# Page loads moved to GpSimd's queue, and memory values projected by token with 512-column weights

## What is computed

```
x = x + 1/2 * SwiGLU_1(RMSNorm(x))
z = RMSNorm(x) @ w_in            # queries, keys, values, gates of three branches
A: attention over paged keys and values (8 heads of 128; each sample has 8 pages of 128 rows)
B: retention (4 heads of 256, a state for each sample)
C: attention into 256 memory tokens (4 heads of 256)
x = x + (sum over branches of sigmoid gate * branch @ w_br) @ w_out
x = x + 1/2 * SwiGLU_2(RMSNorm(x));  y = RMSNorm(x)
```

## Time and profile before

| | |
|---|---|
| median of 3 runs | 2739.36 us |
| the profiled execution | 2738.88 us |
| its span, first to last instruction | 2736.5 us |
| PE busy | 2683.8 us (98%) |
| DVE, ACT, POOL busy | 56%, 40%, 1% |
| granted TensorE clock, mean | 0.994 |
| moved by DMA | 601.19 MB, 220 GB/s |

### The profile page before, as it was taken

How to read it: one execution, slowest core, us unless ns; L and a number is a source line. 1 busy time by engine, 2 the same in 40 slices (tenths; PEclk the granted TensorE clock), 3 DMA queues, 4 the chain that set the end, 5 groups by cost and what they waited for, 6 DMA issues and landing times.

```text
span 2736.5 us, 51767 instructions
## 1 busy us (share of the span) xinstructions
PE 2683.8 (98%) x22179; PEld 2624.4 (96%) x22179; DVE 1540.7 (56%) x2467; ACT 1094.4 (40%) x967; POOL 36.6 (1%) x66
## 2 busy tenths in 40 slices
PE   7999999999999999999997999999999999999998
PEld 7999999999999999998997988899999999999997
DVE  4545554455447778776773744355555555555455
ACT  6433333333335433554452444344433333333345
POOL 0000000000000000000000000000000000000000
PEclk9999999999999999999999999999999999999999
DMA  7575555555555788799987799756555555555553
GB/s 241 179 254 179 184 185 183 178 178 184 185 168 162 237 294 299 251 355 365 324 305 265 268 310 315 279 170 213 173 182 184 183 179 178 183 185 184 177 158 113
DMA packets 502045, 601.19 MB, mean 220 GB/s; under 512 B 12608, under 2 KB 471584, under 8 KB 500576
## 3 DMA queue, kind: packets, MB, share of 16 engines
q1 hardware_dynamic: 485104, 559.08, 62.6%
q0 software_dynamic: 6528, 25.91, 2.6%
q10 hardware_dynamic: 10240, 13.70, 1.4%
HBM read 575.16 MB, written 25.58 MB: 220 GB/s over the span
## 4 chain that ended last, share of the span: by engine, by line
PE 92%; DVE 3%; DMA 3%; ACT 1%; issue 0%; SPq 0%; POOL 0%; DVEq 0%; ACTq 0%; POOLq 0%
PE PS L497 30%; PE PS L498 29%; PE PS L499 29%; DVE splitL L457 2%; DMA ring<-cache_k 1%; PE PS L1845 1%; DMA ring<-cache_mem_k 1%; DMA raw<-w_gate 1%; PE PS L1364 1%; ACT splitH L451 0%; PE PS L1619 0%; PE PS L1587 0%; DMA grow<-b_gate 0%; PE PS L1228 0%; PE PS L1114 0%
## 5 line engine op out<-in xcount | busy, mean ns | idle before, releaser
L457 DVE TENSOR_TENSOR splitL<-raw,splitH 128x2048 fp32r<-128x2048 f32 (+1 forms) x464 | 1011.9, 2181 | 831.0 <-ACT splitH L451 829.8
L451 ACT ACTIVATE splitH<-raw 128x2048 fp32r<-128x2048 f32 (+1 forms) x464 | 847.7, 1829 | 1519.6 <-PE PS L499 1507.4
L497 PE MATMUL PS<-gH,splitH 128*128 128x264 f32 x3072 | 883.0, 287 | 1.8 <-DVE splitL L457 1.8
L498 PE MATMUL PS<-gL,splitH 128*128 128x264 f32 x3072 | 872.8, 284 | 0.0
L499 PE MATMUL PS<-gH,splitL 128*128 128x264 f32 x3072 | 872.5, 284 | 0.0
L497 PEld LDWEIGHTS PS<-gH,splitH 128*128 128x128 f32 x3072 | 580.9, 189 | 21.0 <-issue 20.6
L498 PEld LDWEIGHTS PS<-gL,splitH 128*128 128x128 f32 x3072 | 581.1, 189 | 0.5 <-issue 0.2
L499 PEld LDWEIGHTS PS<-gH,splitL 128*128 128x128 f32 x3072 | 577.9, 188 | 0.0
L497 PE MATMUL PS<-hH,splitH 128*128 128x264 f32 x1536 | 437.7, 285 | 0.0
L498 PE MATMUL PS<-hL,splitH 128*128 128x264 f32 x1536 | 436.4, 284 | 0.0
L499 PE MATMUL PS<-hH,splitL 128*128 128x264 f32 x1536 | 436.2, 284 | 0.0
(11 more groups left out here) (361 smaller groups left out, 3028.0 us busy)
## 6 DMA issues: line engine op xcount, KB each, us to landing
raw<-ffn_w SPq DMA_DIRECT2D x240, 1024.0 KB, 5.1
raw<-w_in SPq DMA_DIRECT2D x64, 1024.0 KB, 7.6
raw<-w_gate SPq DMA_DIRECT2D x48, 1024.0 KB, 5.9
ring<-cache_k SPq DMA_DIRECT2D x64, 512.0 KB, 7.8
ring<-cache_v SPq DMA_DIRECT2D x64, 512.0 KB, 6.1
raw<-ffn_w SPq DMA_DIRECT2D x32, 768.0 KB, 4.7
raw<-w_mem_kv SPq DMA_DIRECT2D x16, 1024.0 KB, 5.9
raw<-w_out SPq DMA_DIRECT2D x16, 1024.0 KB, 5.5
```

Of the source, the lines that this page charges most:

```text
L451: nc.scalar.activation(splitH[:, s, tiles, :], raw[:, u, 0:nk, :], ACT.Copy).then_inc(hi_ready, 1)
L457: nc.vector.tensor_tensor(splitL[:, s, tiles, :], raw[:, u, 0:nk, :], splitH[:, s, tiles, :].bitcast(F32), ALU.subtract).then_inc(split_re ...
L497: nc.tensor.matmul(out, w_hi, H[:, k, 0:n], start=first, stop=False)
L498: nc.tensor.matmul(out, w_hi, L[:, k, 0:n], start=False, stop=False)
```

## The change

- Pages and query rows are loaded by POOL (`pool_pages`), no longer by SP's side work. POOL's list of waits and DMAs becomes `pool_step`, put at chosen slots between the pages. The slots of `LOAD_AT`, the ring and the waits of a page stay.
- Body 1 is made by `sp_values`, `pe_values` and `values_evac`. A unit there is 4 row tiles by 512 columns, so the same 1 MB. The memory tokens' 128 x 128 tiles are now the stationary operand, and the weights move, 512 columns at a time: for each row tile and each of two token tiles three matmuls, 24 in a unit. The result has tokens on partitions; DVE scales it by a number per partition straight into `mvTok0`, two operations of 512 columns in each half.
- `mvT0`, its four turns and their copies are gone. POOL's store of the memory keys and values waits for four copies and the two evacuations.

```diff
+    def sp_values(sp, B, W, col):
+        for c in range(2):
+            for u in range(4):
+                sp_unit_free(sp, B, c, u)
+                sp.dma_start(raw[:, u, :, :].rearrange("p k c -> p (k c)").rearrange("p (k c) -> p k c", k=4),
+                             W[4 * u * P:4 * (u + 1) * P, bass.ds(col + 512 * c, 512)].rearrange("(k p) c -> p k c", p=P)
+                             ).then_inc(raw_full[u], 16)
...
+    def pe_values(pe, B, between):
+        for c in range(2):
+            pe.wait_ge(pair_free[c], 2 * B)
+            for u in range(4):
+                s, _ = split_slot(c, u, UK, False)
+                pe.wait_ge(split_ready, 8 * B + 4 * c + u + 1)
+                for tt in range(2):
+                    out = PS[:, 2 * c + tt, :]
+                    for j in range(4):
+                        k = 4 * u + j
+                        w_hi, w_lo = by_512(splitH[:, s, :, :])[:, j, :], by_512(splitL[:, s, :, :])[:, j, :]
+                        t_hi, t_lo = memH[:, k, tt * P:(tt + 1) * P], memL[:, k, tt * P:(tt + 1) * P]
+                        nc.tensor.matmul(out, t_hi, w_hi, start=u == 0 and j == 0, stop=False)
+                        nc.tensor.matmul(out, t_hi, w_lo, start=False, stop=False)
+                        last = nc.tensor.matmul(out, t_lo, w_hi, start=False, stop=u == 3 and j == 3)
+                last.then_inc(unit_used, 1)
+                between(4 * c + u)
+    def values_evac(dve):
+        def evac(B, c, pr):
+            if pr == 0:
+                return
+            pair_made(dve, B, c, 1)
+            for tt in range(2):
+                nc.vector.tensor_scalar(mvTok0[:, tt, 512 * c:512 * (c + 1)], PS[:, 2 * c + tt, :],
+                                        tsum[:, 3, tt:tt + 1], None, ALU.mult).then_inc(pair_free[c], 1)
+        return evac
...
+    def pool_pages(pool, T):
         for n in range(len(PAGES)):
             kind, b, g = PAGES[n]
             if (kind, b) in QUERY_AT and g == 0 and T == QUERY_AT[kind, b]:
-                sp_query(sp, kind, b)
+                sp_query(pool, kind, b)
             if T == LOAD_AT[n]:
-                sp_page(sp, n)
+                sp_page(pool, n)
...
+    def pool_step(pool, T):
...
+        if T == 71:
+            pool.wait_ge(r_all_done, 1)
+            pool.wait_ge(v_sent, 16)
+            pool.dma_start(mvTok[:, :, :], scratch["mv"].rearrange("(t p) c -> p t c", p=P)).then_inc(mv_in, 16)
+        if T == 72:
+            pool.wait_ge(turn_out, turns_to("va11"))
+            pool.dma_start(mkT[:, :, 0:N_MEM], scratch["mkT"].rearrange("p (a c) -> p a c", a=BT)).then_inc(mk_in, 16)
+            pool.dma_start(o["v_prompt"].rearrange("(t p) c -> p t c", p=P), tokS[:, :, :]).then_inc(v_sent, 16)
+            pool.dma_start(scratch["va"].rearrange("(t p) c -> p t c", p=P), tokS[:, :, :]).then_inc(v_sent, 16)
+        if T == 82:
+            pool_maxima(pool, DKM)
+        if T == 89:
+            pool.wait_ge(a_o, M_HEADS)
+            pool.wait_ge(v_sent, 48)
+            pool.dma_start(vaTok[:, :, :], scratch["va"].rearrange("(t p) c -> p t c", p=P)).then_inc(va_in, 16)
+        if T == 101:
+            pool.wait_ge(m_done, 1)
+            pool.dma_start(biasD[:, :, :].rearrange("p g h -> p (g h)"), scratch["biasD"]).then_inc(biasD_in, 16)
+            bias_rows(pool, 0)
+            bias_rows(pool, 1)
+        if T == 102:
+            pool.wait_ge(unit_used, 8 * (B_GATE + 4))
...
-        sp_wide(sp, 1, d["w_mem_kv"], BR_W)
+        sp_values(sp, 1, d["w_mem_kv"], BR_W)
...
-        pool.wait_ge(kv_out, 8)
+        pool.wait_ge(kv_out, 4)
+        pool.wait_ge(pair_free[0], 4)
+        pool.wait_ge(pair_free[1], 4)
...
+        for T in range(T_END):
+            pool_pages(pool, T)
+            pool_step(pool, T)
...
-        pe_wide(pe, 1, (memH, memL), N_MEM, between=kv_turn_between(pe_kv_turn, pe, 0, (3, 4, 5, 6)))
+        pe_values(pe, 1, kv_turn_between(pe_kv_turn, pe, (3, 4, 5, 6)))
...
-        split_body(dve_split, dve, 1, scaled_evac(dve, mvT0, rmem[:, :], N_MEM))
+        split_body(dve_split, dve, 1, values_evac(dve))
```

More of the change, by code:

```diff
@@ L1022, in dve_start_between, with kv_turn_between @@
         return between
[L1024 removed]
+    def kv_turn_between(turn_one, eng, slots):
         def between(slot):
             if slot in slots:
[L1028 removed]
+                turn_one(eng, slots.index(slot))
         return between
@@ L2234, in sp_side, with bias_rows @@
             if (kind, b) in QUERY_AT and g == 0 and T == QUERY_AT[kind, b]:
-                sp_query(sp, kind, b)
+                sp_query(pool, kind, b)
             if T == LOAD_AT[n]:
-                sp_page(sp, n)
+                sp_page(pool, n)
+    def bias_rows(pool, h):
+        for it in range(2):
+            diag = bass.AP(tensor=scratch["t5"].tensor, offset=h * P * 2 * SEQ + SEQ - 1 - it * P,
+                           ap=[[2 * SEQ - 1, P], [1, SEQ]])
+            pool.dma_start(bias[:, h % 2, it, :], diag).then_inc(bias_in[h % 2], 16)
@@ new lines, in pool_step @@
+    def pool_step(pool, T):
+        if T == 13:
+            pool.wait_ge(pair_free[0], 2 * B_IN + 2)
+            pool.wait_ge(pair_free[1], 2 * B_IN + 2)
+            pool.dma_start(ptab[0:1, :], d["page_table"]).then_inc(pt_in, 16)
+            pool.dma_start(scratch["qaT"], qaT[:, :, :].rearrange("p a c -> p (a c)")).then_inc(qa_kept, 16)
+            pool.wait_ge(turn_out, turns_to("qa1"))
+            pool.dma_start(scratch["qa"], rows_qa[0:DEC, :]).then_inc(qa_kept, 16)
+        if T == 15:
+            pool.wait_ge(qa_kept, 32)
+            pool.wait_ge(rot_done, 1)
+            pool.dma_start(decay[:, :, :], d["decay"]).then_inc(decay_in, 16)
+        if T == 30:
+            pool.wait_ge(turn_out, turns_to("vr1"))
+            pool.dma_start(scratch["vr"], rows_vr[0:DEC, :]).then_inc(vr_kept, 16)
+        for h in range(R_HEADS):
+            if T == RET + 2 * h + 8:
+                pool.wait_ge(s_out, h + 1)
+                pool.dma_start(o["ret_state_prompt"][h].rearrange("(t p) e -> p t e", p=P),
+                               st[:, h % 2, :, :]).then_inc(st_sent[h % 2], 16)
+        if T == 54:
+            pool.wait_ge(pair_free[0], 2 * body_of("ka") + 2)
+            pool.wait_ge(pair_free[1], 2 * body_of("ka") + 2)
+            pool.dma_start(scratch["kaT"], kaT[:, :, :].rearrange("p a c -> p (a c)")).then_inc(k_sent, 16)
+        if T == 56:
+            pool.wait_ge(turn_out, turns_to("ka11"))
+            pool.dma_start(o["k_prompt"].rearrange("(t p) c -> p t c", p=P), tokS[:, :, :]).then_inc(k_sent, 16)
+        if T == 57:
+            pool.wait_ge(turn_out, turns_to("ka1"))
+            pool.dma_start(o["k_sample"], rowsS[0:DEC, :]).then_inc(k_sent, 16)
+        if T == 62:
+            pool.wait_ge(turn_out, turns_to("qm1"))
+            pool.dma_start(scratch["qm"], rowsS[0:DEC, :]).then_inc(qm_kept, 16)
+        if T == 70:
+            pool.wait_ge(turn_out, turns_to("va1"))
+            pool.dma_start(o["v_sample"], rows_va[0:DEC, :]).then_inc(v_sent, 16)
+        if T == 71:
[20 more added lines that the diff above has]
+            pool.wait_ge(unit_used, 8 * (B_GATE + 4))
+            pool.wait_ge(qa_kept, 32)
+            pool.wait_ge(k_sent, 48)
+            pool.dma_start(qaR[:, :, :].rearrange("p a c -> p (a c)"), scratch["qaT"]).then_inc(qk_in, 16)
+            pool.dma_start(kaR[:, :, :].rearrange("p a c -> p (a c)"), scratch["kaT"]).then_inc(qk_in, 16)
+        if T == 107:
+            pool_maxima(pool, DKA)
+        for h in range(2, A_HEADS):
+            if T == MOBA + 3 * (h - 1) + 6:
+                pool.wait_ge(a_p, M_HEADS + h - 1)
+                bias_rows(pool, h)
+        for p in range(2):
+            if T == T_PROJ + 14 + 8 * p:
+                pool.wait_ge(x_kept, 16)
+                pool.wait_ge(mg_lo, 4 * p + 4)
+                pool.dma_start(xT[:, 8 * p:8 * p + 8, :].rearrange("p a c -> p (a c)"),
+                               scratch["x"][:, 8 * p * N:8 * (p + 1) * N]).then_inc(x_back[p], 16)
@@ L2299, in _ @@
[L2299 to L2307, removed]
@@ L2335, in bias_rows @@
[L2335 to L2346, removed]
@@ L2403, in _ @@
         split_body(act_split, act, 0, nothing, between=act_start_between(act))
-        split_body(act_split, act, 1, nothing, between=kv_turn_between(act_kv_turn, act, 0, (3, 4, 5, 6)))
-        split_ffn(act_split, act, B_FFN1, 0, kv_turn_between(act_kv_turn, act, 4, (3, 4, 5, 6)),
+        split_body(act_split, act, 1, nothing, between=kv_turn_between(act_kv_turn, act, (3, 4, 5, 6)))
+        split_ffn(act_split, act, B_FFN1, 0, nothing,
                   lambda i, downs: act_next_h(act, 1, G_MIX, i))
```

59 lines of the change are left out of this document (7 added, 52 removed).

## The result

The changed kernel takes **2719.7 us** (median of 4 runs, 2719.17 to 2724.92) beside 2739.74 of the kernel before in the same comparison: ratio 0.9932, 95% interval 0.9915 to 0.9949, so about 20 us faster. The profiled execution has a span of 2717.2 us and a time of 2719.17, 0.5 under the median. The forecast was 2717, with 2706 to 2736 as its range.

What follows compares the result with a forecast made beforehand. TensorE was taken as the bound, busy 2683.8 of 2736.5 us. Gains of 15 + 0 + 1 + 4.7 + 1.7 = 22.4 us took the median from 2739.36 to 2717 us, with 2706 to 2736 as the 8-in-10 range.

Steps and rivals of the forecast that it cites:

- the loop: 1430 to 1512 us: pages queue behind SyncE's weight loads, which wait for DVE's splits behind earlier page waits; 11.8 us queueing.
- 15 of 19.1 us: 1430 to 1512 us: gain taken from earlier page issue, out of PE's 19.1 us loss; ends 8 and 19.1.
- The 4.9 us for the clock: 1430 to 1512 us: loss from granted clock 0.94, read as one twentieth of the stretch at the lower level.
- DVE's waits under 10 us in total: 1430 to 1512 us: sign of being right, DVE's waits for key pages falling from 43.9 us to under 10.
- the cap that was named: 1430 to 1512 us: at the best rate, 369 GB/s, its 21.90 MB need 59.4 us, limiting how far it shrinks.
- The stage of the stores: 1337 to 1400 us: pages join 3 MB of stores and reloads; 1.2 us idle may go or become 4; 0 taken.
- weights starve: SyncE's queue, 1337 to 1560 us: GpSimd's full queue starves weight loads; slower, 2746 us; chance 0.09.
- the bad stretch: 1430 to 1512 us, 82 us long: 14.2 us PE idle and 4.9 us lower clock, together the 19.1 us prize.
- The stage after: 1512 to 1560 us: weights no longer queue behind value pages; 1 us gain of 3.6 idle, ends -3.6 and +3.
- the present step is set by loading weights, not by columns: Second body: 256-column matmuls take 120.0 ns because of weight loads, so 512 columns save 4.7 us; ends 0 and 5.1.
- The nearest row chosen: Second body: float32 stream, 8 passes of 256 columns at 216 ns each, taken as the price of a 512-column matmul.
- The second set of turns: After the second body: dropping 16 transposes of 128 float32 columns saves 1.7 us of PE.

Runs made afterwards that it cites:

- late pages on GpSimd's queue: The changed kernel, but each page and query load first waits for the split SyncE's queue would have waited for: 2741.3 us, ratio 1.0009.
- Early on SyncE's queue: The kernel before, with page and query loads two slots earlier on SyncE's queue: 2723.1 us; with the 512-column second body as well, 2718.1 us.
- the run with split products: The changed kernel, with one of three products of the second body split by columns (256 and 256, or 384 and 128): 2720.8 us in one execution.
- The corners: Four kernels with the 512-column second body: pages late or early on SyncE's queue (2733.2, 2718.1 us), late or early on GpSimd's (2741.3, 2719.7 us).

## Why the prediction was right, and where it was not

**The bound and the loop.** Right. The gain lies where the prediction looked for it, and 15 of 19.1 us was the size (14.9: PE is idle 10.9 us less, and the same matmuls keep it busy 4.0 us less at the higher clock). The 4.9 us for the clock were near that, though 0.94 means an eighth of the stretch at 1.2 GHz and not a twentieth. The reason for the gain is shown on both sides: pages issued early on either queue take the stretch from 82 to 64 or 67 us, and late pages on GpSimd's queue give the 82 back, with DVE's 43.6 us of waits and the clock of 0.94. The issue 1.25 us after the slot (taken as 1.5) and the granted clock of 1.00 were forecast. *DVE's waits under 10 us in total* was wrong: 19.3 are left. A page needs some 8 us from its free slot to landing (1.27 and 6.75 in the mean of pages 73 to 92), and PE frees the slots of all six pages that DVE waits for, often late. Early on SyncE's queue, with 0.8 and 6.2, DVE still waits 11.7 us. The transfers come near the cap that was named: 339 GB/s in the stretch, beside the best rate of 369.

**The stage of the stores.** Wrong in size: the prediction took 0, with a gain of 1.2 and a loss of 4 as ends, and the run showed a loss of 4.2, just past the bad end. The mechanism had been read from the right row: a full GpSimd queue leaves SyncE's a fifth. The step that failed is the choice of the middle, *the 1.2 us idle may go or become 4; I take 0*, though pages could only be added to that queue there. The run with late pages on GpSimd shows the rival *weights starve* at work in this stage and the one after the bad stretch, where its place had been named: 6.8 and 2.4 us. It did not decide, as early pages were worth more.

**The stage after.** 3.3 us, where 1 was taken (ends -3.6 and +3), so past the good end. ScalarE's wait for the weights of unit 101 is gone, which in the kernel before (1495 to 1560 us) was

```profile
ACT splitH L451 <- DMA raw<-w_gate: 5.8, 1, 5.8
```

These weights land 9.9 us after their issue, where it was 16.5. That SyncE's queue has no value pages in it, as the prediction argued, isn't enough for that: with late pages on GpSimd's queue they take 18.5 us, and nothing is gained. What else it needs stays open.

**Wide matmuls.** The step that failed is *the present step is set by loading weights, not by columns*. It was inferred from 256 columns at 120.0 ns and 264 at 120.5, with weight loads busy throughout. But the step follows the columns from 256 to 512 (117, 175 and 233 ns in the run with split products), and the floor by the weight load lies at some 110 ns. So at 256 columns the weight loads were busy without setting the step. The nearest row chosen, 216 ns of the float32 stream, was not the price: it is 226.6, and the body gives 2.3 us for 4.7. Both bounds that the prediction kept, 0 and 5.1, hold it. At 0.456 ns a column, the price of that run, 264 columns make 120.4, as measured; why 256 took 120.0 in the kernel before and 117 there isn't explained by this.

**The rest.** The second set of turns gave 1.8 us, where 1.7 was taken; the split before each wide unit was in time; everything costed at nothing in the page stages was nothing. The Trainium skill ("DMA: Bandwidth & Descriptors", Specifications) gives a load from GpSimd its first byte at about 1 us, and one from SyncE at about 0.6. The corners agree in sign: pages 73 to 92 land 7.1 us after issue late on GpSimd's queue and 6.7 late on SyncE's, 6.8 and 6.2 early; other transfers beside them count in that too.

**The sum.** 22.4 was forecast, about 20 measured, and 19.7 read stage by stage. Two terms were 2.3 and 2.4 too low or too high in opposite directions, the loss of 4.2 came on top, and a half clock of 1.6 us, absent in this profile by chance, filled part of it. That the total came so near owes something to errors that cancel.

## What to carry to other kernels

When a load is late, measure first how long it stands between the event that allows it and its issue. If that is longer than the transfer, move it earlier in its own queue before giving it another one: one number in a schedule did here what a second queue did, and the second queue brought a price of its own, as its packets took the DMA engines from the weights. Give pages that have time to spare a later slot, above all where stores are in flight; and before widening a matmul, time two widths of it, since busy weight loads do not prove that the weights set the step.

## What the runs showed that was not expected

- The rounded-float32 matmul's step follows its columns from 256 up (117, 175 and 233 ns for 256, 384 and 512), though a weight load precedes every one of them. The floor by that load shows only at 128 columns, and one matmul later: 60 ns, and 50 more in the step behind.
- TensorE's half clock in the first FFN (173.9 to 177.3 us before), 1.6 us a time, comes and goes between executions without a change in the work ahead of it. A difference of that size between two profiles can be that alone.
- The same pages through GpSimd's queue instead of SyncE's cost 8.1 us when they were issued about as late.
